# Where the operands of TensorE's matmuls stand in SBUF: activations on a 1280-byte pitch, weight slots 32 bytes apart

## The reference

```python
def run_trunk(x, ...):
    for i in range(2):
        h = rms_norm(x, w['norm_mix'][i])
        x = x + mixer(h)                     # projection in, recurrence, projection out
        x = x + peer_ffn(rms_norm(x, w['norm_ffn'][i]), w_q, sub_keys, u, v)
def peer_ffn(x, w_q, sub_keys, u, v):
    q = x @ w_q                              # scores of 2 x 128 keys a head, top 16 of 256
    act = gelu(einsum('thed,td->the', u[e], x))
    return einsum('the,thed->td', softmax(top_s) * act, v[e])
```

## Time and profile before

| what | value |
|---|---|
| runs before, median of 3 | 2508.62 us (2504.9 to 2510.07) |
| span of the profiled execution, first to last instruction | 2507.1 us |
| TensorE clock granted over the span | 0.958 of 2.4 GHz |
| PE busy | 2330.1 us (93%) |
| POOL, DVE, ACT busy | 1669.8, 1713.6, 1112.0 us |
| moved by DMA | 370.27 MB, mean 148 GB/s |

### The profile page before, as it was taken

The page is one execution under the profiler, slowest core; times in us unless marked ns, Lnnn a source line. Parts: engine busy times, 40 slices in busy tenths (PEclk is TensorE's granted clock), DMA queues, the critical chain, the costliest instruction groups (busy, mean ns, idle before and its releaser), DMA issues. The chain is left out here.

```text
span 2507.1 us, 46304 instructions
## 1 busy us (share of the span) xinstructions
PE 2330.1 (93%) x19024; PEld 2217.5 (88%) x19024; DVE 1713.6 (68%) x2773; ACT 1112.0 (44%) x1893; POOL 1669.8 (67%) x716
## 2 busy tenths in 40 slices
PE   6977978999999999999979875899999999999998
PEld 5957858999999999999979722899999999999998
DVE  4776553795678268888868376349767762888887
ACT  4512234455554444444446412344555444444443
POOL 4714016687666788888867544758766668888885
PEclk9978988999999999999989977899999999999999
DMA  4410013454444555555535443445544445555553
GB/s 156 153 52 34 35 44 135 144 185 160 144 144 144 169 184 178 184 178 184 179 123 169 157 151 109 133 137 163 176 146 147 145 147 182 180 182 181 181 182 131
DMA packets 102226, 370.27 MB, mean 148 GB/s; under 512 B 15392, under 2 KB 15744, under 8 KB 98816
## 3 DMA queue, kind: packets, MB, share of 16 engines
q1 hardware_dynamic: 102016, 367.30, 45.4%
HBM read 352.67 MB, written 14.58 MB: 146 GB/s over the span
## 5 line engine op out<-in xcount | busy, mean ns | idle before, releaser
L355 POOL TENSOR_TENSOR weights_halves<-weights_raw,weights_halves 128x1024 fp32r<-128x1024 f32 x638 | 1541.6, 2419 | 571.1 <-ACT weights_halves L347 570.8
L347 ACT CAST weights_halves<-weights_raw 128x1024 fp32r<-128x1024 f32 x638 | 669.9, 1051 | 936.2 <-PE peer L378 482.6
L860 DVE TENSOR_TENSOR gated<-acts,gated 128x264 fp32r<-128x264 f32 x256 | 615.3, 2405 | 127.5 <-ACT gated L742 127.5
L378 PE MATMUL peer<-ffn_in_hi,weights_halves 128*128 128x264 f32 x4608 | 650.7, 288 | 14.9 <-ACT ffn_in_hi L271 14.9
L378 PEld LDWEIGHTS peer<-ffn_in_hi,weights_halves 128*128 128x128 f32 x4608 | 590.9, 189 | 22.0 <-issue 16.6
L364 PE MATMUL peer<-gated,weights_halves 128*128 128x264 f32 x2048 | 583.2, 285 | 0.0
L362 PE MATMUL peer<-gated,weights_halves 128*128 128x264 f32 x2048 | 581.2, 284 | 0.0
L363 PE MATMUL peer<-gated,weights_halves 128*128 128x264 f32 x2048 | 579.9, 283 | 0.0
L363 PEld LDWEIGHTS peer<-gated,weights_halves 128*128 128x128 f32 x2048 | 385.9, 188 | 0.0
L362 PEld LDWEIGHTS peer<-gated,weights_halves 128*128 128x128 f32 x2048 | 385.4, 188 | 0.0
L364 PEld LDWEIGHTS peer<-gated,weights_halves 128*128 128x128 f32 x2048 | 384.4, 188 | 0.0
(11 more groups left out here) (465 smaller groups left out, 2359.3 us busy)
## 6 DMA issues: line engine op xcount, KB each, us to landing
weights_raw<-in_up SPq DMA_DIRECT2D x256, 512.0 KB, 3.5
weights_raw<-in_down SPq DMA_DIRECT2D x256, 512.0 KB, 3.5
weights_raw<-in_ssm_w_in SPq DMA_DIRECT2D x40, 512.0 KB, 3.4
weights_raw<-in_w_q SPq DMA_DIRECT2D x32, 512.0 KB, 3.4
weights_raw<-in_ab_w_in SPq DMA_DIRECT2D x30, 512.0 KB, 3.5
weights_raw<-in_ssm_w_out SPq DMA_DIRECT2D x16, 512.0 KB, 3.5
states<-in_ssm_in SPq DMA_DIRECT2D x8, 1024.0 KB, 7.4
ssm_sample<-states SPq DMA_DIRECT2D x8, 1024.0 KB, 4.8
```

Source lines behind the costliest of these rows:

```text
L347: act.copy(self.halves[:, 0, slot, :], self.raw[:, slot, :]).then_inc(self.hi_made, 1)
L355: pool.tensor_tensor(self.halves[:, 1, slot, :], self.raw[:, slot, :], self.halves[:, 0, slot, :].bitcast(F32), ALU.subtract).then_inc(sel ...
L378: ins = pe.matmul(out, self.halves[:, half, n % RING, at], both[side], start=start and half == 0 and side == 0 and k == 0, stop=stop and h ...
L860: core.gated_lo.inc(dve.tensor_tensor(a_lo[:, j % RING, :], acts[:, j, :], a_hi[:, j % RING, :].bitcast(F32), ALU.subtract))
```

## The change

No instruction is added, removed or moved on any engine; the instructions stand in the same order, and what differs is where in SBUF their operands lie.

- `lanes` allocates the moving operands with a pitch of 320 elements (1280 bytes = 5 x 256) from an address that is 224 modulo 256. All of `ffn_in`, `mix_in`, `out`, `y` (hi and lo) and the ring of gated rows then start at 224 modulo 256. The same holds for all 15,312 matmuls of the tile stream.
- The six slots of weight halves get a pitch of 1032 elements (4128 bytes = 16 x 256 + 32). In the built program the three hi slots start at 160, 192 and 224 modulo 256, the three lo slots at 0, 32 and 64.
- To make room, the constant `index_row` shrinks from 128 to 16 elements, and in the second mixer's way out `root` and `squares` lie in `z`, which is no longer needed there.

```diff
+LINE = 256
+LANE_AT = 224
+LANE = 320
+TILE_STEP = D_MODEL + 8
...
+    def lanes(self, ctx, name, n):
+        gap = (LANE_AT - self.nc.sbuf_base) % LINE // 32 * 32
+        if gap:
+            self.sb(ctx, name + "_gap", [P, gap // 4])
+        return self.sb(ctx, name, [P, n, LANE], F32R)[:, :, 0:T]
...
-    core.index_row = core.sb(ctx, "index_row", [P, P])
+    core.index_row = core.sb(ctx, "index_row", [P, 16])
...
-            link(pool.iota(core.index_row, [[1, P]], base=0, channel_multiplier=0,
+            link(pool.iota(core.index_row, [[1, 16]], base=0, channel_multiplier=0,
...
-        self.room, self.halves = core.shared(ctx, "weights_halves", [P, 2, RING, D_MODEL], F32R)
+        self.room, halves = core.shared(ctx, "weights_halves", [P, 2 * RING * TILE_STEP], F32R)
+        self.halves = halves.rearrange("p (a r w) -> p a r w", a=2, r=RING)[:, :, :, 0:D_MODEL]
...
-        h_hi = core.sb(ctx, "ffn_in_hi", [P, KC, T], F32R)
-        h_lo = core.sb(ctx, "ffn_in_lo", [P, KC, T], F32R)
+        h_hi = core.lanes(ctx, "ffn_in_hi", KC)
+        h_lo = core.lanes(ctx, "ffn_in_lo", KC)
...
-        a_ring = a_ring[:, 0:2 * RING * T].rearrange("p (a r t) -> p a r t", a=2, r=RING)
+        a_ring = a_ring[:, 0:2 * RING * LANE].rearrange("p (a r t) -> p a r t", a=2, r=RING)[:, :, :, 0:T]
...
-                y_hi = core.sb(tail, "y_hi", [P, INNER_TILES, T], F32R)
-                y_lo = core.sb(tail, "y_lo", [P, INNER_TILES, T], F32R)
-                root = core.sb(tail, "root", [P, GROUPS, T])
-                ssm_out(core, par, xdt, y, y_hi, y_lo, root, x, first + SSM_TILES, core.sb(tail, "squares", [P, KC, T]))
+                y_hi = core.lanes(tail, "y_hi", INNER_TILES)
+                y_lo = core.lanes(tail, "y_lo", INNER_TILES)
+                root = z[:, KC:KC + GROUPS, :]
+                ssm_out(core, par, xdt, y, y_hi, y_lo, root, x, first + SSM_TILES, z[:, 0:KC, :])
```

More of the change, by code:

```diff
@@ L1898, in mixer_ab @@
                 h = core.sb(inner, "mix_in", [P, KC, T])
-                h_hi = core.sb(inner, "mix_in_hi", [P, KC, T], F32R)
-                h_lo = core.sb(inner, "mix_in_lo", [P, KC, T], F32R)
+                h_hi = core.lanes(inner, "mix_in_hi", KC)
+                h_lo = core.lanes(inner, "mix_in_lo", KC)
                 room = Room(temp["logs4"].rearrange("p n a t -> p (n a t)"))
@@ L1930, in mixer_ab @@
             with ExitStack() as end:
-                out_hi = core.sb(end, "out_hi", [P, KC, T], F32R)
-                out_lo = core.sb(end, "out_lo", [P, KC, T], F32R)
+                out_hi = core.lanes(end, "out_hi", KC)
+                out_lo = core.lanes(end, "out_lo", KC)
                 heads = core.sb(end, "heads", [P, HEAD_MASKS, P])
```

## The result

The kernel became slower: 2514.89 us (median of 8 runs, 2511.33 to 2520.9) against 2508.48 us before (8 runs, 2504.9 to 2510.07), a ratio of 1.003 with a 95% interval of 1.002 to 1.004. The prediction said 2469 us and faster; the time lies inside its range and outside the likeliest case's own range. The profiled execution after spans 2510.7 us, 3.6 us more than that of before.

What follows compares the result with a forecast made beforehand. PE's matmul stream was taken as the bound, losing 11 ns per matmul at full clock. Operands at 224 gave -40 us, weight places and the rest nothing: 2508.6 - 40 = 2469 us, range 2410 to 2525, likeliest case 2440 to 2495.

Steps and rivals of the forecast that it cites:

- What bounds it: Tile stream: PE busy without a break at full clock, 11 ns per matmul lost over the columns' 110 ns.
- the lower bound of 110 ns: Tile stream: least possible gap, the half-clock row scaled to full clock; 11.2 ns off each matmul, -159 us.
- Moving operands at 224, -40 us: Tile stream: 14,184 paying matmuls at a gap of 118.4 ns, -2.8 ns each, -40 us.
- Its second way, by tiles: Down-stage tiles: 24 operands at 224 would gain 0.105 us of 2.925, giving 117.5 ns and about -50 us.
- Six places for the weights, nothing: Weight slots, before all at 96: another place's effect isn't in the trace, so nothing was taken.
- The rest, nothing: Second mixer's way out, `index_row`, reuse of `z`: nothing taken, up to +2 us for casts as separate rows.
- The distance to the weights decides: Rival, tile stream: weight-to-operand distance sets the gap, 121.5 ns, +8 us, 2517 us, up to 2565; chance 0.26.
- the settled pass: Up stage before the change: eight blocks' gaps ran from 116 ns (at 224) to 126 ns (at 64), 120.9 a matmul.
- Nothing changes: Rival, tile stream: gaps only shift starts, the mean is set elsewhere; 2508 us, within 5; chance 0.22.
- The settled 116 holds: Rival, tile stream: 116 ns always or better, -74 us or more, 2435 us and down to 2350; chance 0.16.

Runs made afterwards that it cites:

- the column experiment: The change, with the second pass of each tile in up-stage order cut to 248 columns and the third to 200; 2468.39 us, one run.
- The first experiment: Moving operands at 224 as in the change, all six weight slots left at 96 as in the kernel before; 2533.75 us, ratio 1.011.
- the shift by 64: The change with operands and weights all moved by 64 bytes, distances kept; 2513.56 us, ratio 1.0021.
- the eight distances: The change with all six weight slots at one place, a different distance in each kernel; from 2489.31 us (distance 224) to 2577.28 us (distance 96).

## Why the prediction was wrong

**What bounds it: right.** PE is busy without a break before, after and in every experiment's window, and the count of matmuls in that window follows the gap. Some 11 ns are lost at full clock over the columns, and the column experiment shows that these lie on top of the columns. But they are mostly not to be had: no distance of the eight went below 120.0 ns, so 10 of the 11 ns stayed at every one, and no run came near the lower bound of 110 ns.

**Moving operands at 224, -40 us: the step that failed.** It took 118.4 ns, the mean of gaps after an operand at 224 among other places, as the price of a stream of nothing else. The first experiment is that stream with the weights where they were: 123.3 ns and +26 us (2533.75 against 2507.38). The gap of one matmul in a mixture is no price of its place; the prediction saw short gaps paid back in the earlier trace rows and took a mean over the states, but all these states belong to mixtures, and the pure stretch has its own. Its second way, by tiles, fell with the same fault: the slot with 224 in the earlier trace rows was faster as a mixture.

**Six places for the weights, nothing: wrong as well.** Beside operands packed as before it holds for the time (0.9991). Beside operands at 224 it is worth 2514.89 - 2533.75 = -19 us: it takes the tiles off distance 128. So the change is +26 and then -19, and about +7 is left, near the +6.4 measured.

**The rest, nothing: right**, by the unchanged rows on DVE, POOL and `y_hi`.

**The rivals.** "The distance to the weights decides" named the cause, as the shift by 64 and the eight distances show, and its 2517 us is close, by luck (its 121.5 ns comes to 121.6 by its own figures, and its +8 us to +9). Its prices were wrong, for they came from the settled pass: it held 128 for good and 224 for bad, the reverse of the table. It expected the long gaps with lo weights, and in slot 1's down tiles those are the longest, 127 ns, but at distance 192, which alone gives 120.0: its sign was right by another way. "Nothing changes" missed too, by a little: 6.4 us where it gave 5. By the Trainium skill's page SBUF — State Buffer (Who interferes with whom), TensorE waits on nobody, and its two read ports are independent; the eight runs don't agree, with 2371 to 2503 matmuls in 300 us by the relative place of the two operands, though no run shows whether the ports are where it happens. "The settled 116 holds" is refuted by 123.3.

**How the loss is made up.** By A, the plain mean of single distances, two thirds hi and one third lo, slot 0 should take 24 x (2 x 120.95 + 120.0) / 3 = 2.895 us in the down stage, slot 1 2.916 and slot 2 2.915; measured are 2.889, 2.965 and 2.913. Two slots are within 6 ns and slot 1 is 49 ns over. In the up stage A gives 2.886, 2.915 and 2.913 us where 2.897, 2.920 and 2.897 are measured: off by up to 16 ns one by one, and right in the mean. So most of the change is a mean of good and bad distances that happens to fall near the mixture of before, and its excess is one combination, (32, 192) in the change's order of slots; in a ring of its own the same pair took 2.933. The stream accounts for some 3 of the 6.4 us between the medians. The two profiled executions are 3.6 us apart: by the starts of their tiles, that of after loses 2.8 us in the up and down stages and 2.5 in the second mixer's first projection, and gains 1.7 elsewhere. What is not in the tiles comes and goes, and I find two such things in the second mixer's first stretch. One is the half clock shown above. The other is a wait of 3.4 us of PE for DVE: before and after both have it (PE busy 36.10 and 36.05 of 40 us), while the profiled execution of the arrangement shifted by 64, whose tiles are those of after, has neither:

```profile
1340.00:1380.00 40.00, 39.50 (x322) 38.82 (x322) 30.71 (x60) 26.86 (x54) 32.20 (x14) 1.00 0.54 180
```

It took 2506.08 us; the ten runs of that arrangement lie at 2506.08 to 2508.96 (four) and 2512.92 to 2517.21 (six), so I take these two for the difference between the groups, though only one execution of it was traced. The mean clock granted over the span, which is on record for every run, goes with them: 0.957 to 0.958 in the four, 0.954 to 0.956 in the six. It is 0.954 to 0.956 in all eight runs of the change too, and 0.956 to 0.959 before. So about half of the 6.4 us lies outside the tiles and goes with a lower clock; whether the change makes that likelier is open.

**Open.** Why a distance costs what it does, and whether it is that to the weights in use or to those that load meanwhile: every kernel with one place has both the same. Writes of other engines into SBUF are an unlikely reason: at distance 96 each gap of a tile is 126 or 127 ns, while POOL writes for 2.40 of its 3.04 us and ACT's cast lasts 1.05. A pure stretch can also settle at two lengths: in the first experiment the tiles of the first mixer's way out took 2.880 us, and nearly all others 2.96; at distance 0 those of both ways out took mostly 2.880, and others 2.912. At 224 and 192 every stage settled at 2.880.

## What to carry to other kernels

A gap between pipelined instructions measured in a mixture is not the price of that instruction: before it is multiplied by a count, run a stretch that holds nothing else. In a kernel like this one, where every matmul loads its own weights, count the matmuls in a stretch where PE never waits for one arrangement of addresses after the other, with one distance modulo 256 from weights to operand throughout; here 224 or 192 gave 120.0 ns and 96 gave 126.7. Slots at places of their own turn one distance into a mixture, whose price no single distance tells.

## What the runs showed of the hardware that was not expected

- In a long stretch of one distance, the distance modulo 256 between the two operands of a matmul in SBUF moves the gap of the stream from 120.0 to 126.7 ns, for 264 fp32r columns with 128 x 128 weights loaded each time; shifting both by 64 changes nothing (down tiles equal to 1 ns).
- From 264 to 248 columns the gap falls by 6.75 ns, with 11 ns over the columns at either width; at 200 columns the pass's mean is 109.0 ns, 26 ns over them.
- A tile's length depends on what ran before it: with only slot 1's weights moved, slot 0's down tiles, two tiles behind, went from 2.889 to 2.928 us, and repeat another group of three gaps at the same addresses.
- Executions of one program lie in groups some 8 us apart (2499.24 to 2500.22 and 2504.61 to 2507.66 us with only slot 1 moved). At distances 224 and 192, with the same tiles of 2.880 us, the profiled spans are 2483.3 and 2497.9 us; in 1340:1380 PE got through 324 matmuls at a clock of 1.00 in the one and 278 at 0.96 in the other, busy for 39.44 and 36.03 us.
